# Order of the high and low weight products within a unit, and of the input chunks at the last gate, in a two-block layer on one core

## The chip, the cores and the metric

The kernel runs on one core of one Trainium2 chip. The time is the device time of one execution in microseconds (us), for one launch of the whole program. All times of the trace are counted from the start of the profiled span.

## What is computed

Two transformer blocks follow each other for 256 tokens of width 2048. Nearly all the work is in products of the activations with weights that are read once. What matters for the change, cut from the reference:

```python
# first block
z = h @ w_in                                   # 2048 x 12304
merged = sigmoid(m_a) * (y_a @ w_proj_a) + sigmoid(m_b) * (y_b @ w_proj_b)
y = merged @ w_out
...                                            # cross attention: wq, wk, wv, wo
hid = conv(h @ w_up)                           # 2048 x 11264
y = (gelu(gate) * up) @ w_down                 # 5632 x 2048
# second block
u = h @ w_in_2
q, k, v, z_attn, q_idx, k_idx, w_idx, z_ssd, xbc, dt_raw = split(u)
o_attn = dsa_attention(q, k, v, q_idx, k_idx, w_idx) * silu(z_attn)
o_ssd = ssd_mixer(xbc, z_ssd, dt_raw)          # gated, group-normed
mixed = concatenate([o_attn, o_ssd])           # chunks 0 to 7 and 8 to 15 of 128
out = layer_norm(ALPHA * h + mixed @ w_out_2)
```

## The kernel before, in words

The products keep float32 accuracy from a rounded format: each weight and each activation is held as a high part and a low part. Three products stand for one: high by high, low weight by high activation, high weight by low activation.

**Groups and units.** `groups_of` lists the matrix products as groups of output columns in the order of execution. A group is cut along its input dimension into units of `chunk` times 128 rows (a chunk of the input is 128 rows). A unit is 1 MB of weights in most cases. SyncE loads it into one of three `raw` buffers, ScalarE copies it rounded into `wh` (`split_hi`, semaphore `s_hi`), VectorE subtracts to get `wl` (`split_lo`, semaphore `s_lo`), and TensorE multiplies; at the end of a unit it raises `s_used`, which frees the buffers. ScalarE and VectorE prepare unit n + 2 while TensorE works at n. Units follow the list strictly on every engine.

**Three kinds.** In a "feat" group (256 output columns, units of 8 chunks) the weights are stationary. The activations' high and low halves lie side by side in `xt`, so one product of 512 moving columns does high weight by both parts, and one of 256 columns does low weight by the high part. There are 96 such groups of 16 chunks and 8 of 8 chunks (`pa`), which with two blocks of 128 output columns make 96 x 32 + 8 x 16 = 3200 pairs of one 512-column and one 256-column product. In a "tok" group (512 output columns, units of 4 chunks) the activations are stationary and all three products have 512 moving columns. Of "thin" groups there are two (`glr` and `kiw`), with three products of 256 columns for each chunk.

**The order inside a unit** is written in `block_products` (L940 to L975): for each chunk and block, the high product (or products) and the low product follow each other at once. At a unit's start TensorE waits for `s_lo`, thus for both halves of the weights. In a group's last unit block 0 is finished first, so that its evacuation can begin, and then block 1 (`products`).

**Work beside.** The table `BESIDE` names, for a unit and a slot, what is done between: slot 1 is ahead of unit 1, slot 1.5 is in its middle (on TensorE, ahead of the products of chunk nk // 2). All engines read the same table, so it fixes the order of their queues.

**The end of the second block.** `za0` to `za3` are the four groups of the attention's gate (two units each), `w20` to `w23` the output projection (four units each, input `mix`). The attention part of the mixed input (chunks 0 to 7) comes from `mix_attn`, which multiplies the gate and writes `xth` and `xtl`; it needs the gate's own group finished. The state-space part (chunks 8 to 15) comes from `mix_ssd`: TensorE transposes `xs`, and ScalarE and VectorE copy it scaled into the same `xt`. Both overwrite what `za3` reads, so they wait for `s_used` of `za3`. `ssd_norm` on VectorE finishes `xs` beside `za2`. In the kernel before, `w20` takes its chunks 0 to 15 in order; the two halves of `mix_ssd` stand in the middle of its units 0 and 1.

**Where an input is used first**, `block_products` waits for each chunk by itself (`ready`). Such places that matter here are `xo0` (the output of the cross attention, 4 chunks) and `ug0_0` (the first group of the wide layer; half of its input is transposed at slot 0.5 of its first unit, `h3_b`).

Of the kernel before, what the change touches and what calls it, by code (L numbers as in the profile page):

```python
# [13 lines left out]
KC = D // 128  # L14
# [56 lines left out]
class Group:  # L71


    def __init__(self, name, w, kcs, cols, kind, x, chunk=4, k_off=0, late=0):
        self.name, self.w, self.kcs, self.cols, self.kind, self.x = name, w, kcs, cols, kind, x
        self.chunk, self.k_off, self.late = chunk, k_off, late
        self.width = sum(c for _, c in cols)


class Unit:  # L80


    def __init__(self, n, gi, ui, k, nk, g):
        self.n, self.gi, self.ui, self.k, self.nk, self.g = n, gi, ui, k, nk, g
        self.last = k + nk == g.kcs
        self.m = nk * g.width


# [24 lines left out]
def groups_of(I):  # L113
    w_in, w2, up, down = I["w_in"][0], I["w_in_2"][0], I["ffn_w_up"][0], I["ffn_w_down"][0]
    out = []

    def add(*a, **k):
        out.append(Group(*a, **k))

    for i in range(2):  # L120
        add("vs%d" % i, w_in, KC, [(1024 + 512 * i, 512)], "tok", "h1")
    for i in range(4):
        add("u%d" % i, w_in, KC, [(256 * i, 256)], "feat", "h1", chunk=8)
    for i in range(8):
        add("ma%d" % i, w_in, KC, [(8208 + 256 * i, 256)], "feat", "h1", chunk=8)
    for i in range(8):
        add("pa%d" % i, I["w_proj_a"][0], 8, [(256 * i, 256)], "feat", "ya", chunk=8)
    add("glr", w_in, KC, [(8192, 16)], "thin", "h1", chunk=16)
    for i in range(4):
        add("q%d" % i, w_in, KC, [(2048 + 256 * i, 256)], "feat", "h1", chunk=8)  # L130
    for i in range(4):
        add("k%d" % i, w_in, KC, [(3072 + 256 * i, 256)], "feat", "h1", chunk=8)
    for i in range(4):
        add("v%d" % i, w_in, KC, [(4096 + 512 * i, 512)], "tok", "h1")
    for i in range(4):
        add("og%d" % i, w_in, KC, [(6144 + 512 * i, 512)], "tok", "h1")
    for i in range(8):
        add("mb%d" % i, w_in, KC, [(10256 + 256 * i, 256)], "feat", "h1", chunk=8)
    for i in range(8):
        add("pb%d" % i, I["w_proj_b"][0], KC, [(256 * i, 256)], "feat", "yb", chunk=8)  # L140
    for i in range(4):
        add("wo%d" % i, I["w_out"][0], KC, [(512 * i, 512)], "tok", "mg")
    for i in range(2):
        add("xk%d" % i, I["xa_wk"][0], KC, [(256 * i, 256)], "feat", "mem", chunk=8)
    for i in range(2):
        add("xq%d" % i, I["xa_wq"][0], KC, [(256 * i, 256)], "feat", "h2", chunk=8)
    add("xv", I["xa_wv"][0], KC, [(0, 512)], "tok", "mem")
    for i in range(4):
        add("xo%d" % i, I["xa_wo"][0], 4, [(512 * i, 512)], "tok", "ox", late=3 * (i == 3))
    for half in range(2):  # L150
        for i in range(HF // 2):
            c0 = half * HF * 128 + 256 * i
            add("ug%d_%d" % (half, i), up, KC, [(c0, 256)], "feat", "h3", chunk=8)
            add("uu%d_%d" % (half, i), up, KC, [(FF + c0, 256)], "feat", "h3", chunk=8)
        for i in range(4):
            add("dn%d%d" % (half, i), down, HF, [(512 * i, 512)], "tok", "ac", k_off=half * HF,
                late=2 * (half == 1 and i == 3))
    add("qi0", w2, KC, [(2560, 512)], "tok", "h4")
    add("kiw", w2, KC, [(3584, 80), (6704, 48)], "thin", "h4", chunk=16)
    add("qi1", w2, KC, [(3072, 512)], "tok", "h4")  # L160
    add("kv", w2, KC, [(1024, 512)], "tok", "h4")
    for i in range(8):
        add("xb%d" % i, w2, KC, [(4688 + 256 * i, 256)], "feat", "h4", chunk=8)
    for i in range(2):
        add("q2%d" % i, w2, KC, [(512 * i, 512)], "tok", "h4")
    for i in range(2):
        add("zs%d" % i, w2, KC, [(3664 + 512 * i, 512)], "tok", "h4")
    for i in range(4):
        add("za%d" % i, w2, KC, [(1536 + 256 * i, 256)], "feat", "h4", chunk=8)
    for i in range(4):  # L170
        add("w2%d" % i, I["w_out_2"][0], KC, [(512 * i, 512)], "tok", "mix")
    return out


def units_of(groups):
    units = []
    for gi, g in enumerate(groups):
        for ui, k in enumerate(range(0, g.kcs, g.chunk)):
            units.append(Unit(len(units), gi, ui, k, min(g.chunk, g.kcs - k), g))
    return units  # L180

# [43 lines left out]
}  # L225

# [29 lines left out]
def build(nc, I, cst_d, out_d):  # L256
# [210 lines left out]
    def hi_count(n):  # L467
        return n + 4
# [26 lines left out]
    for stage in plan:  # L495
        for _ in range(BANKS.get(stage, 0) + WARM.get(stage, 0)):
            b = taken % 4
# [55 lines left out]
    def tensor_program(p):  # L553

        def mm(out, l, r, start, stop, share=False):
            return p.matmul(out, l, r, start=start, stop=stop, skip_group_check=share)  # L556
# [383 lines left out]
        def block_products(u, order, begin=True):  # L940

            g, s, nc_ = u.g, u.n % 3, u.g.width
            pset = ps[u.gi % 2]
            xh, xl = operand[g.x]
            h3 = v3(wh[s][:, 0:u.m], nc_)
            l3 = v3(wl[s][:, 0:u.m], nc_)
            if begin and u.n:
                p.wait_ge(s_lo, hi_count(u.n))
            if begin and u.ui == 0 and accfree_base[g.name]:
                p.wait_ge(s_accfree[u.gi % 2], accfree_base[g.name])  # L950
            for b, kk in order:
                if kk == u.nk // 2 and b == 0:
                    run_beside(u, u.ui + 0.5)
                kg = u.k + kk
                if b == 0 and first_use[g.name]:
                    p.wait_ge(*ready(g.x, kg, int(g.k_off > 0)))
                if b == 0 and u.n == 0:
                    p.wait_ge(s_lo, kk + 1)
                first, final = kg == 0, kg == g.kcs - 1
                if g.kind == "tok":  # L960
                    t_ = slice(b * 128, b * 128 + 128)
                    o = pset[b][:, 0:nc_]
                    mm(o, xh[:, kg, t_], h3[:, kk, :], first, False)
                    mm(o, xh[:, kg, t_], l3[:, kk, :], False, False)
                    t = mm(o, xl[:, kg, t_], h3[:, kk, :], False, final)
                elif g.kind == "thin":
                    o = pset[0][0:nc_, 0:256]
                    mm(o, h3[:, kk, :], xh[:, kg, :], first, False)
                    mm(o, h3[:, kk, :], xl[:, kg, :], False, False)
                    t = mm(o, l3[:, kk, :], xh[:, kg, :], False, final)  # L970
                else:
                    c = slice(b * 128, b * 128 + 128)
                    mm(pset[b], h3[:, kk, c], pair(g.x, kg), first, False, share=True)
                    t = mm(pset[b][:, 0:256], l3[:, kk, c], xh[:, kg, :], False, final, share=True)
            return t  # L975

# [32 lines left out]
    def scalar_program(a):  # L1009
# [336 lines left out]
        def mix_attn(tiles):  # L1346
            for i in tiles:
                c = slice(2 * i, 2 * i + 2)
                heard()
                a.wait_ge(s_used, after("za3") - (i < 3))  # L1350
                to_v.add(act(xth[:, c, :], v3(zz[i], 256), ACT.Copy))

        def mix_ssd(k0):
            a.wait_ge(s_used, after("za3"))
            split_turned(use["mix_ssd%d" % k0], lambda k: VT[:, 76 + k:77 + k], k0, xth[:, 8:16, :])

        def evac_w2(i, blocks):
# [120 lines left out]
    def vector_program(v):  # L1478
# [847 lines left out]
        def mix_attn(tiles):  # L2326
            for qb in range(2):
                free(use["at_out%d" % qb][0])
                free(use["at_out%d" % qb][1])
            for i in tiles:  # L2330
                z3 = v3(zz[i], 256)
                c = slice(2 * i, 2 * i + 2)
                heard(last["za%d" % i])
                to_act.add(tt(z3, z3, oaT[:, c, :], ALU.mult))
                heard()
                v.wait_ge(s_used, after("za3") - (i < 3))
                lo_part(xtl[:, c, :], z3, xth[:, c, :]).then_inc(s_mixa, 1)

        def mix_ssd(k0):
            v.wait_ge(s_used, after("za3"))  # L2340
            split_turned(use["mix_ssd%d" % k0], lambda k: VT[:, 76 + k:77 + k], k0, xth[:, 8:16, :], xtl[:, 8:16, :])

        def evac_w2(i, blocks):
# [314 lines left out]
```

## Time and profile before

| | us |
|---|---|
| three runs, median | 2126.94 |
| three runs, lowest and highest | 2124.58, 2134.12 |
| the profiled execution | 2129.74 |
| its span in the trace | 2127.9 |
| mean granted TensorE clock | 0.997 of 2.4 GHz |
| TensorE, products | 2094.1 (98% of the span) |
| TensorE, loading of stationary operands | 1779.3 (84%) |
| VectorE | 1396.8 (66%) |
| ScalarE | 956.1 (45%) |
| DMA queue of the weights | 54.4% of 16 engines |

The profiled execution has 1.84 us outside its span, and is 2.80 us above the median of the three runs. TensorE's busy time is made of modelled ends that overlap (a 512-column product is drawn 0.39 us long and the next one starts after 0.23 us), so the distance from one start to the next is the number that tells what a product costs; it is read from the timeline, or from a window's length over the number of products in it.

### The profile page before, as it was taken

The page shows a single profiled execution, that of the slowest core. Times are in us where ns is not written, and L with a number is a line of the kernel's source. Part 1 is how long each engine was busy: PE and PEld are TensorE (multiplying, and loading weights), DVE is VectorE, ACT ScalarE, POOL GpSimd, SP SyncE. Part 2 cuts the span into 40 slices and gives each one's busy share as a digit, 9 for nine tenths or more (in the row PEclk, how much of TensorE's full clock was granted, in tenths as well). Part 3 has the DMA queues.
Part 4 walks back from the last instruction along what each step waited for, and adds up shares of the span by engine and source line. Part 5 has one row for each costly group of instructions (what it writes and reads, how often), then busy time and mean ns, then how long its engine had stood idle before and what let it go on. Part 6 is the DMA issues. An engine that isn't in the chain of part 4 may idle for free.

```text
span 2127.9 us, 26265 instructions
## 1 busy us (share of the span) xinstructions
PE 2094.1 (98%) x11051; PEld 1779.3 (84%) x11051; DVE 1396.8 (66%) x1566; ACT 956.1 (45%) x927; POOL 26.7 (1%) x42
## 2 busy tenths in 40 slices
PE   8999999999999999999999999999999999999996
PEld 6888888878888888878888888888888888888885
DVE  5665676454556667677777545777754668887765
ACT  5444253234443445464444433444443434445542
POOL 2000000000000000000000000000000000000001
PEclk9999999999999999999999999999999999999998
DMA  8555556445666565445655556556555554554462
GB/s 286 178 183 182 178 159 198 155 162 179 180 190 223 202 234 198 159 133 184 198 179 177 198 189 205 172 185 198 180 203 201 168 178 140 191 165 156 126 238 93
DMA packets 299140, 388.49 MB, mean 183 GB/s; under 512 B 12720, under 2 KB 217860, under 8 KB 297872
## 3 DMA queue, kind: packets, MB, share of 16 engines
q1 hardware_dynamic: 296288, 374.50, 54.4%
q0 software_dynamic: 2560, 12.26, 1.5%
q8 instruction: 87, 1.43, 0.3%
q14 instruction: 29, 0.24, 0.0%
q10 hardware_dynamic: 176, 0.07, 0.0%
HBM read 384.71 MB, written 2.10 MB: 182 GB/s over the span
## 4 chain that ended last, share of the span: by engine, by line
PE 93%; DVE 4%; ACT 1%; issue 1%; DMA 0%; SPq 0%; DVEq 0%; ACTq 0%
PE ps L556 89%; PE pm L556 4%; PE pm L559 1%; DVE wl L1483 1%; ACT wh L1014 1%; DVE y L1483 1%; DMA raw<-in_w_in 0%; DVE xt L1491 0%; DVE vs L1483 0%; ACT xt L1014 0%; DVE yaf L1483 0%; DVE xx L1491 0%; ACT L1014 0%; ACT yaT L1014 0%; DVE uT L1638 0%
## 5 line engine op out<-in xcount | busy, mean ns | idle before, releaser
L1483 DVE TENSOR_TENSOR wl<-raw,wh 128x2048 fp32r<-128x2048 f32 (+1 forms) x361 | 805.0, 2243 | 454.6 <-ACT wh L1014 454.2
L556 PE MATMUL ps<-xt,wh 128*128 128x512 f32 (+2 forms) x2816 | 983.4, 396 | 1.7 <-DVE xt L1491 1.0
L1014 ACT ACTIVATE wh<-raw 128x2048 fp32r<-128x2048 f32 (+1 forms) x361 | 671.2, 1873 | 572.0 <-PE ps L556 567.4
L556 PE MATMUL ps<-xt,wl 128*128 128x256 f32 (+1 forms) x2784 | 779.7, 280 | 0.0
L556 PEld LDWEIGHTS ps<-xt,wh 128*128 128x128 f32 (+1 forms) x2816 | 524.9, 187 | 132.1 <-issue 3.9
L556 PEld LDWEIGHTS ps<-xt,wl 128*128 128x128 f32 (+1 forms) x2784 | 523.8, 188 | 0.5
L556 PE MATMUL ps<-wh,xt 128*128 128x512 f32 x1600 | 504.2, 393 | 1.7 <-DVE xt L1483 1.1
L556 PEld LDWEIGHTS ps<-wh,xt 128*128 128x128 f32 x1600 | 300.5, 188 | 66.5 <-issue 1.8
L556 PE MATMUL ps<-wl,xt 128*128 128x512 f32 x800 | 311.5, 389 | 0.0
L556 PEld LDWEIGHTS ps<-wl,xt 128*128 128x128 f32 x800 | 150.4, 188 | 31.1 <-issue 1.0
L556 PE MATMUL ps<-wh,ach 128*128 128x512 f32 x352 | 137.1, 389 | 0.0
L556 PE MATMUL ps<-wh,acl 128*128 128x512 f32 x352 | 136.9, 389 | 0.0
L556 PE MATMUL ps<-wl,ach 128*128 128x512 f32 x352 | 136.9, 389 | 0.0
L1014 ACT ACTIVATE cv<-up,vt 128x256 f32<-128x256 f32 x88 | 51.3, 602 | 157.4 <-DVE up L1638 157.2
L1491 DVE SCALAR_TENSOR_TENSOR cv<-up,vt,cv 128x255 f32<-128x255 f32 (+1 forms) x176 | 81.2, 482 | 33.0 <-ACT cv L1014 29.8
L556 PE MATMUL ps<-ybT,wh 128*128 128x512 f32 x256 | 88.8, 394 | 0.0
L556 PEld LDWEIGHTS ps<-wh,ach 128*128 128x128 f32 x352 | 66.1, 188 | 13.8
L556 PEld LDWEIGHTS ps<-wh,acl 128*128 128x128 f32 x352 | 66.1, 188 | 13.8
L556 PEld LDWEIGHTS ps<-wl,ach 128*128 128x128 f32 x352 | 66.1, 188 | 13.5
L556 PE MATMUL ps<-ybT,wl 128*128 128x256 f32 x256 | 70.9, 277 | 0.0
L1638 DVE TENSOR_REDUCE up<-ps 128x256 f32<-128x512 f32 x88 | 58.6, 686 | 5.9 <-PE ps L556 5.8
L556 PEld LDWEIGHTS ps<-ybT,wh 128*128 128x128 f32 x256 | 48.0, 188 | 11.1
(323 smaller groups left out, 1366.9 us busy)
## 6 DMA issues: line engine op xcount, KB each, us to landing
raw<-in_w_in SPq DMA_DIRECT2D x147, 1024.0 KB, 5.3
raw<-in_ffn_w_up SPq DMA_DIRECT2D x88, 1024.0 KB, 5.3
raw<-in_ffn_w_down SPq DMA_DIRECT2D x40, 1024.0 KB, 5.1
raw<-in_w_out SPq DMA_DIRECT2D x32, 1024.0 KB, 5.1
raw<-in_w_proj_b SPq DMA_DIRECT2D x16, 1024.0 KB, 5.3
raw<-in_w_proj_a SPq DMA_DIRECT2D x8, 1024.0 KB, 5.3
raw<-in_xa_wk SPq DMA_DIRECT2D x4, 1024.0 KB, 5.1
raw<-in_xa_wq SPq DMA_DIRECT2D x4, 1024.0 KB, 5.2
```

Of the source, the lines that this page charges most:

```text
L556: return p.matmul(out, l, r, start=start, stop=stop, skip_group_check=share)
L559: return p.transpose(out, a, ident)
L1014: return a.activation(out, in_, func, bias=bias, scale=scale)
L1483: return v.tensor_tensor(out, a, b, op)
L1491: return v.scalar_tensor_tensor(out=out, in0=a, scalar=s, in1=b, op0=op0, op1=op1)
L1638: v.tensor_reduce(out, halves, AX.X, ALU.add).then_inc(s_accfree[set_of[name]], 1)
```

## The change

Inside a unit, all products with the high weights come first, for all chunks and blocks of the call, and then all products with the low weights. TensorE waits for `s_hi` at the unit's start and for `s_lo` between the two halves. In "tok" groups the high half thus has two products for each chunk and block, the low half one. The number of products, loads and columns is the same. A group's first product is now told by the unit and not by the chunk number, so that chunks can be taken in another order.

`za3` and `w20` take the input chunks 8 to 15 first. `mix_ssd` moves from the middle of units 0 and 1 of `w20` to the start and the middle of `za3`'s second unit, and waits for one unit less of `za3`; `mix_attn0` moves to `w20`'s unit 0 and `mix_attn3` to its unit 1.

```diff
@@ class Unit
-        self.last = k + nk == g.kcs
+        self.last = (ui + 1) * g.chunk >= g.kcs
@@ groups_of
-        add("za%d" % i, w2, KC, [(1536 + 256 * i, 256)], "feat", "h4", chunk=8)
+        add("za%d" % i, w2, KC, [(1536 + 256 * i, 256)], "feat", "h4", chunk=8, k_first=8 * (i == 3))
...
-        add("w2%d" % i, I["w_out_2"][0], KC, [(512 * i, 512)], "tok", "mix")
+        add("w2%d" % i, I["w_out_2"][0], KC, [(512 * i, 512)], "tok", "mix", k_first=8 * (i == 0))
@@ units_of
-        for ui, k in enumerate(range(0, g.kcs, g.chunk)):
+        for ui, k in enumerate(list(range(g.k_first, g.kcs, g.chunk)) + list(range(0, g.k_first, g.chunk))):
@@ BESIDE
-    ("za3", 1): ["mix_attn0"], ("w20", 0): ["mix_attn3"], ("w20", 0.5): ["mix_ssd0"], ("w20", 1.5): ["mix_ssd4"],
+    ("za3", 1): ["mix_ssd0"], ("za3", 1.5): ["mix_ssd4"], ("w20", 0): ["mix_attn0"], ("w20", 1): ["mix_attn3"],
@@ tensor_program, block_products
             if begin and u.n:
-                p.wait_ge(s_lo, hi_count(u.n))
+                p.wait_ge(s_hi, hi_count(u.n))
...
                 if b == 0 and u.n == 0:
+                    p.wait_ge(s_hi, kk + 1)
+                first = u.ui == 0 and kk == 0
+                t_, c = slice(b * 128, b * 128 + 128), slice(b * 128, b * 128 + 128)
+                if g.kind == "tok":
+                    mm(pset[b], xh[:, kg, t_], h3[:, kk, :], first, False)
+                    mm(pset[b], xl[:, kg, t_], h3[:, kk, :], False, False)
+                elif g.kind == "thin":
+                    mm(pset[0][0:nc_, 0:256], h3[:, kk, :], xh[:, kg, :], first, False)
+                    mm(pset[0][0:nc_, 0:256], h3[:, kk, :], xl[:, kg, :], False, False)
+                else:
+                    mm(pset[b], h3[:, kk, c], pair(g.x, kg), first, False, share=True)
+            if begin and u.n:
+                p.wait_ge(s_lo, hi_count(u.n))
+            for b, kk in order:
+                kg = u.k + kk
+                if b == 0 and u.n == 0:
                     p.wait_ge(s_lo, kk + 1)
-                first, final = kg == 0, kg == g.kcs - 1
+                final = u.last and kk == u.nk - 1
+                t_, c = slice(b * 128, b * 128 + 128), slice(b * 128, b * 128 + 128)
                 if g.kind == "tok":
...
-                    mm(o, xh[:, kg, t_], h3[:, kk, :], first, False)
-                    mm(o, xh[:, kg, t_], l3[:, kk, :], False, False)
-                    t = mm(o, xl[:, kg, t_], h3[:, kk, :], False, final)
+                    t = mm(pset[b], xh[:, kg, t_], l3[:, kk, :], False, final)
...
                 else:
...
-                    mm(pset[b], h3[:, kk, c], pair(g.x, kg), first, False, share=True)
                     t = mm(pset[b][:, 0:256], l3[:, kk, c], xh[:, kg, :], False, final, share=True)
@@ scalar_program and vector_program, mix_attn (a. and v.)
-                a.wait_ge(s_used, after("za3") - (i < 3))
+                a.wait_ge(s_used, after("za3"))
@@ scalar_program and vector_program, mix_ssd (a. and v.)
-            a.wait_ge(s_used, after("za3"))
+            a.wait_ge(s_used, after("za3") - 1)
```

## Rows read from the trace of the kernel before

**Rows 1.** The page, busy time, share of the span, instructions.

```profile
PE 2094.1 (98%) x11051; PEld 1779.3 (84%) x11051; DVE 1396.8 (66%) x1566; ACT 956.1 (45%) x927; POOL 26.7 (1%) x42
```

**Rows 2.** The page, chain that ended last, shares by engine.

```profile
PE 93%; DVE 4%; ACT 1%; issue 1%; DMA 0%; SPq 0%; DVEq 0%; ACTq 0%
```

**Rows 3.** The chain in order of time, wide layer: start, us, what.

```profile
937.47 728.64 PE ps L556 x3832
```

**Rows 4.** Windows: stretch, length, then busy (x count) by engine, PEclk, DMA.

```profile
280.00:340.00 60.00, 60.00 (x342) 51.99 (x341) 46.49 (x40) 29.91 (x16) 0.00 (x0) 1.00 0.58 177
...
600.00:720.00 120.00, 120.00 (x694) 104.93 (x693) 78.17 (x64) 45.48 (x31) 1.09 (x2) 1.00 0.65 209
950.00:1170.00 220.00, 220.00 (x1247) 190.80 (x1246) 160.66 (x174) 106.35 (x97) 0.00 (x0) 1.00 0.57 183
1200.00:1290.00 90.00, 90.00 (x398) 74.51 (x397) 41.38 (x24) 32.18 (x19) 0.00 (x0) 1.00 0.58 194
1310.00:1540.00 230.00, 230.00 (x1305) 199.40 (x1304) 167.68 (x181) 109.04 (x101) 0.00 (x0) 1.00 0.56 183
```

**Rows 5.** Timeline, TensorE, the thin group kiw: start, us, what.

```profile
1703.62 0.28 PE L556 MATMUL ps<-xt,wl 128*128 128x256 f32 x1
1703.74 0.40 PE L556 MATMUL ps<-xt,wh 128*128 128x256 f32 x2
...
1709.03 0.28 PE L556 MATMUL ps<-xt,wl 128*128 128x256 f32 x1
```

**Rows 6.** Timeline, TensorE, the thin group glr.

```profile
250.35 0.40 PE L556 MATMUL ps<-xt,wh 128*16 128x256 f32 x2
...
251.06 0.40 PE L556 MATMUL ps<-xt,wh 128*16 128x256 f32 x2
```

**Rows 7.** Timeline, TensorE, unit starts between 92 and 138 us.

```profile
92.81 0.28 PE L556 MATMUL ps<-xt,wl 128*128 128x256 f32 x1
93.47 0.51 PE L556 MATMUL ps<-xt,wh 128*128 128x512 f32 x1 [0.38 <-DVE wl L1483]
93.81 0.28 PE L556 MATMUL ps<-xt,wl 128*128 128x256 f32 x1
...
99.11 0.28 PE L556 MATMUL ps<-xt,wl 128*128 128x256 f32 x1
99.46 0.50 PE L556 MATMUL ps<-xt,wh 128*128 128x512 f32 x1
...
136.72 0.28 PE L556 MATMUL ps<-xt,wl 128*128 128x256 f32 x1
137.19 0.50 PE L556 MATMUL ps<-xt,wh 128*128 128x512 f32 x1 [0.18 <-DVE wl L1483]
```

**Rows 8.** Timeline, VectorE and TensorE, from the last gate into the output projection.

```profile
2008.41 2.36 DVE L1483 TENSOR_TENSOR xs<-xs,st 128x1024 f32<-128x1024 f32 x2
...
2018.89 0.68 DVE L1483 TENSOR_TENSOR zk<-zk,oaT 128x512 f32<-128x512 f32 x1
...
2020.88 0.69 DVE L1483 TENSOR_TENSOR zk<-zk,oaT 128x512 f32<-128x512 f32 x1
...
2021.12 0.47 PE L556 MATMUL ps<-wh,xt 128*128 128x512 f32 x1
...
2030.74 0.60 PE L559 MATMUL pm<-cst,xs 128*128 128x128 f32 x4
...
2032.13 0.50 PE L556 MATMUL ps<-wh,xt 128*128 128x512 f32 x1 [0.79 <-DVE xt L1483]
```

**Rows 9.** Timeline, TensorE, first units of ug0_0 and of xo0.

```profile
934.38 0.28 PE L556 MATMUL ps<-xt,wl 128*128 128x256 f32 x1
935.04 0.30 PE L559 MATMUL pm<-cst,yA 128*128 128x128 f32 x1 [0.39 <-DVE yA L1487]
...
900.58 0.40 PE L556 MATMUL ps<-wh,oxl 128*128 128x512 f32 x1
900.99 0.51 PE L556 MATMUL ps<-wh,oxh 128*128 128x512 f32 x1
```

More of the change, by code:

```diff
@@ L71, with __init__ @@
 class Group:
-    def __init__(self, name, w, kcs, cols, kind, x, chunk=4, k_off=0, late=0):
+    def __init__(self, name, w, kcs, cols, kind, x, chunk=4, k_off=0, late=0, k_first=0):
         self.name, self.w, self.kcs, self.cols, self.kind, self.x = name, w, kcs, cols, kind, x
-        self.chunk, self.k_off, self.late = chunk, k_off, late
+        self.chunk, self.k_off, self.late, self.k_first = chunk, k_off, late, k_first
         self.width = sum(c for _, c in cols)
@@ L957, in block_products @@
                 if b == 0 and u.n == 0:
+                    p.wait_ge(s_hi, kk + 1)
[14 more added lines that the diff above has]
+                if b == 0 and u.n == 0:
                     p.wait_ge(s_lo, kk + 1)
-                first, final = kg == 0, kg == g.kcs - 1
+                final = u.last and kk == u.nk - 1
+                t_, c = slice(b * 128, b * 128 + 128), slice(b * 128, b * 128 + 128)
                 if g.kind == "tok":
-                    t_ = slice(b * 128, b * 128 + 128)
-                    o = pset[b][:, 0:nc_]
-                    mm(o, xh[:, kg, t_], h3[:, kk, :], first, False)
-                    mm(o, xh[:, kg, t_], l3[:, kk, :], False, False)
-                    t = mm(o, xl[:, kg, t_], h3[:, kk, :], False, final)
+                    t = mm(pset[b], xh[:, kg, t_], l3[:, kk, :], False, final)
                 elif g.kind == "thin":
[L967 to L970, printed above, removed]
-                else:
-                    c = slice(b * 128, b * 128 + 128)
-                    mm(pset[b], h3[:, kk, c], pair(g.x, kg), first, False, share=True)
+                    t = mm(pset[0][0:nc_, 0:256], l3[:, kk, :], xh[:, kg, :], False, final)
+                else:
                     t = mm(pset[b][:, 0:256], l3[:, kk, c], xh[:, kg, :], False, final, share=True)
@@ L2335, in mix_attn @@
                 heard()
-                v.wait_ge(s_used, after("za3") - (i < 3))
+                v.wait_ge(s_used, after("za3"))
                 lo_part(xtl[:, c, :], z3, xth[:, c, :]).then_inc(s_mixa, 1)
         def mix_ssd(k0):
-            v.wait_ge(s_used, after("za3"))
+            v.wait_ge(s_used, after("za3") - 1)
             split_turned(use["mix_ssd%d" % k0], lambda k: VT[:, 76 + k:77 + k], k0, xth[:, 8:16, :], xtl[:, 8:16, :])
```

## The prediction

> **What bounds the kernel now.** I read the page first. TensorE is busy for 98% of the span, VectorE for 66% [rows 1], and the chain that ended last lies on TensorE for 93% [rows 2]. So a change can gain in two ways: the few waits of TensorE go, or a product costs less. A product's cost is not its drawn length. It is the distance between starts, and a window over a stretch of products alone gives it: length over count, less the two or so that lap over the edges.
>
> A stretch of 512-column products gives 90.00 / 396.5 = 0.227 us each. For the pairs of the feat groups (one of 512 and one of 256 columns) four windows give 60 / 340 = 0.1765, 220 / 1245 = 0.1767 and 230 / 1303 = 0.1765 us a product, thus 0.353 a pair, but 120 / 692 = 0.1734, or 0.3467 a pair, between 600 and 720 us; the granted clock is 1.00 in all [rows 4]. The same pair has two prices. What would the two cost apart? The only 256-column products in a row with a 128-column load ahead of each are those of kiw: from 1703.62 to 1709.03 there are 15 triples, 5.41 / 45 = 0.1202 us each [rows 5]. And 0.2267 + 0.1202 = 0.3469: the cheaper price is the sum of the parts, and the dearer one has 0.0066 us on top, which comes with the alternation, since neither the runs of 512 columns nor those of 256 show it.
>
> **The change part by part.**
>
> *Grouping by length (feat).* It neither adds nor removes a product or a load: 3200 pairs, in half-units of up to 16 equal products. Price after: 0.2267 for a high product. In the trace such runs have activations stationary and weights moving, here it is the other way round; I take the same price, because the pair's own sum fits. For a low product, bounds: kiw's 0.1202, and below it glr's 0.1183 (from 250.35 to 251.06, six products [rows 6]), which has 16 stationary columns and is thus less like. The other end is no gain, the pair at 0.353. I take kiw's, since shape and load are the same. Gain: I let the window at 280 us stand for u, ma, pa, q and k (20 groups of 32 pairs and 8 of 16: 768) and those at 950 and 1310 us for ug and uu (44 groups: 1408), in all 2176 x 0.0066 = 14.4 us. The other 1024 pairs are at the cheap price where the window at 600 us looks, and the dear price must end somewhere ahead of it; I add a guess of 0.9. So **15.3 us**, ends 0 and, with glr's price, 15.3 + 3200 x 0.0019 = 21.4.
>
> By the Trainium skill, "TensorE: Matmul & The Clock Gate", section "Back-to-back issue gap", a product costs its columns over 2.4 GHz and 2.5 ns. An estimate from that page is 0.216 + 0.109 = 0.325 us a pair in any order, so that grouping gives nothing; the trace disagrees with both numbers, since it has 0.347 and 0.353.
>
> *Grouping in tok.* All three products have 512 columns before and after, 0.227 each. Nothing; the end on either side is a hundredth of a microsecond a unit, 3 us at most, since in the long stretches all neighbours of such a product have its length already.
>
> *The second wait in each unit.* 361 units now have one more wait. What is queued behind it is only TensorE's own low half. A wait that is already fulfilled costs nothing where rows show it: the 3832 products from 937.47 to 1666.11 contain 135 unit starts, each with its wait, and at 0.353 a pair and 0.227 a product the stretch is filled to about 0.1 us [rows 3, 4]. Behind a wait that does hold, the next product starts about 0.11 us late as well (93.47 to 93.81 is 0.34 in place of 0.23 [rows 7]). I take 0; ends 0 and 361 x 0.11 = 40 us.
>
> *Waiting for the high weights only.* Three unit starts are late because of `wl`: 93.47, 99.46 and 137.19 [rows 7]. Against the 0.12 of the low product before them they lose 0.54, 0.23 and 0.35, and 0.11 each behind. After the change `wl` is wanted 16 x 0.227 = 3.6 us later, so these **1.4 us** go. VectorE stays as loaded as it was, so what is late next there is its evacuations, and they have nobody waiting within that half unit.
>
> *The last gate and w20.* TensorE stands from about 2031.2 (four transposes from 2030.74 on, 0.11 each) to 2032.13, and loses 0.11 behind it: it wants chunks 6 and 7 of the mixed input, which VectorE writes last [rows 8]. After, w20 begins with chunks 8 to 15. Moved: two times 8 transposes on TensorE, 8 copies each on ScalarE and VectorE, no DMA; `xs` is ready at 2008.41 + 2.36 = 2010.8, and za3's second unit starts at 2021.12 - 5.55 = 2015.6, so the transposes don't wait. The copies are queued on VectorE ahead of `wl` for w20's unit 1, which is wanted some 9 us after w20's start. mix_attn then has the two units 0 and 1, 24 x 0.227 = 5.4 us each, for four tiles whose products on VectorE follow each other by 2.0 us (2018.89 to 2020.88 [rows 8]) and two splits between. Gain **1.0 us**. The loads of the last norm's vectors on POOL's queue wait for mix_ssd4 and start earlier, which nobody needs. If VectorE were later than that, unit 2 of w20 would wait in the place of unit 1.
>
> *What is lost.* A half-unit of high products runs through the chunks faster than before, so an input that is late is met sooner, and the low products that used to fill the time come after it. At ug0_0 the transposes of slot 0.5 wait for `yA` until 935.04 [rows 9]; four chunks' low products, 8 x 0.12 = 1.0 us, no longer lie ahead of them. At xo0 two low products of 0.23 move behind the wait that ends at 900.99 [rows 9]: 0.4 us. Together **1.4 us lost**.
>
> Sum: 15.3 + 1.4 + 1.0 - 1.4 = **16.3 us**. The profiled execution of 2129.74 (span 2127.9 and 1.84 around it) would come to 2113.4. It lies 2.80 above the median of the runs, and against that the forecast is 2126.94 - 16.3 = **2110.6**.
>
> **The rivals.**
>
> *A: the pair keeps its price.* The 0.0066 us might not come from alternation but from something else of these stretches, and go with high runs just the same. For it: the same alternation is cheap at 600 us [rows 4], so alternation alone does not make it, and the page's order-free rule would also give no gain. Against it: tok runs at 1200 us, between two dear stretches, are at 0.227 [rows 4]. Then only the waits and the losses are left, 1.4 + 1.0 - 1.4 = 1.0, and the time is 2125.9.
>
> *B: the second wait costs.* The middle wait parts the loading ahead of the low products from the high ones in front. If each costs the 0.11 us of a fill, it is 40 us, and the time 2126.94 - 16.3 + 40 = 2151. The side flips to slower by over 0.5% (10.6 us) from (16.3 + 10.6) / 361 = 0.075 us a wait. Against it stands the stretch of 135 waits at no cost [rows 3].
>
> *C: the low half is bound by its loads.* Each low product needs a fresh load, drawn 1779.3 / 11051 = 0.161 us long on average [rows 1]; in a run there is no 512-column product to hide it. If a low product took 0.161, it would be 3200 x 0.041 = 131 us more, and 2242. kiw's 0.120 speaks plainly against it [rows 5]. By the Trainium skill, same page, section "LDWEIGHTS (loading the stationary operand)", a load of 128 columns takes an estimated 107 ns; kiw's step is above that and cannot part the load from the product.
>
> **How the numbers follow.** The forecast has 0.74, with an own range from 2106 to 2116 (glr's price on one side, a third of the gain missing on the other). A has 0.15, B 0.08, C 0.02, and 0.01 is left for the order at the end turning into a longer wait. A measurement of this kernel can tell about 0.5%, 10.6 us. Faster by more than that takes the forecast to hold for at least two thirds, 0.75; the same 0.15 (A), slower 0.10 (B and C). The forecast's own range holds about 0.7, so to hold 8 in 10 the range has to reach to A: 2105 to 2126.5.
>
> **What would show it.** In the changed profile a window within 950 to 1160 should have 0.1734 us a product, and the timeline low products in runs of 0.120 and high ones in runs of 0.227. The first low product behind the last high one should start 0.227 after it; 0.34 there means B. The wait at 2032 should be gone, those on `wl` before 140 us too, and the one on `yA` near 935 about 1 us longer. A pair still at 0.353 means A. The forecast is wrong if the chain shows TensorE in one piece through the wide layer and the piece is not about 9 us shorter than 728.6.

## The result and the profile after

The change made the kernel faster, by a little less than half of what was forecast (7.6 us between the medians, 16.3 forecast): the median of 11 runs is 2122.14 us (2119.56 to 2122.74), that of the kernel before in 11 runs 2129.78 (2123.17 to 2134.12). The ratio is 0.9963, with a 95% interval of 0.9952 to 0.9974, thus 0.26% to 0.48% faster, where the forecast was 2110.6 us or 0.8%. The profiled execution took 2122.14 us, its span is 2120.4. Two things strike at once. The gain is within the 0.5% that the forecast called "the same", and the runs of the kernel before are spread over 11 us, those of the changed one within 3.2. The size of the gain depends on these runs: the kernel before was run again beside the experiments, 25, 17 and 11 times, with medians of 2127.29, 2127.91 and 2129.38 us, and the changed kernel's median lies 5.2 to 7.2 us below those.

The page of the changed kernel, busy times and the chain's shares [rows 1, 2]:

```profile
PE 2086.7 (98%) x11051; PEld 1788.6 (84%) x11051; DVE 1395.0 (66%) x1566; ACT 953.8 (45%) x927; POOL 26.5 (1%) x42
...
PE 97%; DVE 2%; DMA 0%; ACT 0%; issue 0%; SPq 0%; DVEq 0%; ACTq 0%
```

TensorE has 97% of the chain instead of 93%. That is not a measure of time saved: the waits found gone below come to some 2.4 us, a tenth of a per cent of the span, so most of the four points are a chain that takes another way through the same work. What the kernel's time hangs on is TensorE's own pace.

The windows of the changed kernel, with the columns of [rows 4]:

```profile
280.00:340.00 60.00, 60.00 (x344) 52.80 (x343) 47.08 (x41) 30.24 (x17) 0.00 (x0) 1.00 0.60 182
600.00:720.00 120.00, 120.00 (x686) 105.64 (x686) 76.78 (x64) 46.12 (x33) 1.09 (x2) 1.00 0.65 210
950.00:1160.00 210.00, 210.00 (x1207) 185.22 (x1206) 154.62 (x168) 101.12 (x94) 0.00 (x0) 1.00 0.58 186
```

And the wide layer in its chain in order of time [rows 3]:

```profile
936.48 722.88 PE ps L556 x3840
```

210 / 1205 = 0.1743 us a product is 0.3485 a pair. The forecast's test was 0.1734, or 0.3467. The piece of the chain is 5.8 us shorter than the 728.64 of before, where the forecast's sign was about 9. The counts at 280 and 600 us give 0.3509, which is too dear: such a window begins and ends inside runs, and the one at 600 us holds 348 long products but 337 short ones. A group's start and the next one's are surer, here two pb groups in TensorE's timeline of the changed kernel:

```profile
649.33 3.82 PE L556 MATMUL ps<-ybT,wh 128*128 128x512 f32 x16
...
660.48 0.86 PE L556 MATMUL ps<-ybT,wh 128*128 128x512 f32 x3
```

11.15 us for 32 pairs is 0.3485 there too, **dearer** than the 0.3467 of before. So the grouped order has one price in all these stretches, between the two that the kernel before had.

Where the missing 0.0018 a pair sits shows the timeline of the changed kernel, TensorE, from one unit of the wide layer into the next. Each row is a run of equal products; its cost is the distance to the next start, not the drawn length:

```profile
1001.42 3.82 PE L556 MATMUL ps<-xt,wh 128*128 128x512 f32 x16
1005.08 2.08 PE L556 MATMUL ps<-xt,wl 128*128 128x256 f32 x16
1006.99 2.00 PE L556 MATMUL ps<-xt,wh 128*128 128x512 f32 x8
1008.83 1.11 PE L556 MATMUL ps<-xt,wl 128*128 128x256 f32 x8
```

The 16 high products take 3.66 us and not 3.627 (16 x 0.2267), the 8 take 1.84 and not 1.813: both 0.03 too long, whatever the run's length. The low runs take 1.91 and 0.95, a hundredth less than 16 and 8 times 0.120. In the single starts of the trace, read to the nanosecond, the first five high products behind a low run of 8 or 16 are 0.234, 0.236, 0.228, 0.232 and 0.231 apart, and from the sixth on 0.227; the first low product follows after 0.227 and is itself 0.007 short. So a **passage** from low products to high ones costs 0.028 - 0.007 = 0.021 us net. A group of two units has three, 0.06 us: 32 x 0.3467 + 0.06 = 11.153 us, which is what every full feat group of the changed kernel takes that follows another one and has no wait or other work in it.

The waits. At 93 and at 99 us the high products now follow at once, [rows 7] had 0.54 and 0.23 us there:

```profile
92.77 1.36 PE L556 MATMUL ps<-xt,wl 128*128 128x256 f32 x10
93.97 2.00 PE L556 MATMUL ps<-xt,wh 128*128 128x512 f32 x8
...
98.60 1.11 PE L556 MATMUL ps<-xt,wl 128*128 128x256 f32 x8
99.55 0.63 PE L556 MATMUL ps<-xt,wh 128*128 128x512 f32 x2
```

The step from 92.77 to 93.97 is ten low products at 0.120. The last gate passes into w20 without a break (TensorE's timeline; [rows 8] had the transposes at 2030.74 and the wait up to 2032.13):

```profile
2009.18 1.03 PE L559 MATMUL pm<-cst,xs 128*128 128x128 f32 x8
2009.97 1.17 PE L556 MATMUL ps<-xt,wh 128*128 128x512 f32 x4
2010.98 1.04 PE L559 MATMUL pm<-cst,xs 128*128 128x128 f32 x8
...
2015.57 1.11 PE L556 MATMUL ps<-xt,wl 128*128 128x256 f32 x8
2016.52 3.82 PE L556 MATMUL ps<-wh,xt 128*128 128x512 f32 x16
```

The two losses came as worked out: at ug0_0 and at xo0 TensorE now waits where low products had lain [rows 9]:

```profile
899.53 0.49 PE L556 MATMUL ps<-wh,oxh 128*128 128x512 f32 x1 [0.47 <-DVE oxl L1491]
...
934.05 0.30 PE L559 MATMUL pm<-cst,yA 128*128 128x128 f32 x1 [1.33 <-DVE yA L1495]
```

And one thing that was not in the forecast: in the window from 262 us the granted clock is 0.72 on average.

```profile
262.00:268.00 6.00, 6.00 (x23) 4.73 (x22) 4.12 (x6) 0.69 (x1) 0.00 (x0) 0.72 0.44 125
```

From 264.0 to 267.4 it was at its lower level (1.2 GHz), and products of 512 columns were 0.427 apart. Ahead of it TensorE had run two lots of four small products (gate2_2 and gate2_3, 256 columns each) with only four high products between. Five other profiled executions have the same order there (e2, e4, e5, e6, e8 below) and did not fall there. The same steps of 0.427 stand at the very start, from 17.2 to 21.7, where the kernel before was at 0.227 from 17.6 on.

**The account between the two profiled executions**, by group starts: up to 66 us 1.45 lost (the slow start); 66 to 248 us 3.6 gained (pairs from 0.353 to 0.3485, and the three waits); to 270 us 1.3 lost (the clock); to 580 us 1.4 gained; 580 to 728 us 0.8 **lost** (0.3467 to 0.3485); xo0 and ug0_0 0.5 and 0.9 lost; the wide layer's rest 3.2 and 3.4 gained; xb 0.4 lost; the end 1.2 gained. Together 7.5, the difference of the spans.

### The profile page after: what moved, and what is told of

Read it like the earlier page. It is cut to its first block, busy times and chain, and to the rows that moved or that the text cites. A ratio compares the mean times of both kernels' runs of the same rounds, so it can differ in the third digit from the quotient of the medians.

```text
span 2120.4 us, 26265 instructions
## 1 busy us (share of the span) xinstructions
PE 2086.7 (98%) x11051; PEld 1788.6 (84%) x11051; DVE 1395.0 (66%) x1566; ACT 953.8 (45%) x927; POOL 26.5 (1%) x42
## 4 chain that ended last, share of the span: by engine, by line
PE 97%; DVE 2%; DMA 0%; ACT 0%; issue 0%; SPq 0%; DVEq 0%; ACTq 0%
PE ps L556 92%; PE pm L556 4%; PE pm L559 1%; DVE y L1491 1%; DMA raw<-in_w_in 0%; DVE xx L1499 0%; DVE xt L1499 0%; ACT junkB L1042 0%; ACT xt L1022 0%; DVE wl L1491 0%; DVE yA L1495 0%; SPq L2532 0%; ACT y L1022 0%; DVE xt L1491 0%; DVE bst L2361 0%
## 5 line engine op out<-in xcount | busy, mean ns | idle before, releaser
L556 PE MATMUL ps<-xt,wh 128*128 128x512 f32 (+2 forms) x2816 | 684.7, 390 | 1.0 <-DVE xt L1499 1.0
L556 PEld LDWEIGHTS ps<-xt,wh 128*128 128x128 f32 (+1 forms) x2816 | 507.5, 188 | 98.1 <-issue 3.9
L556 PE MATMUL ps<-wh,xt 128*128 128x512 f32 x1600 | 390.6, 394 | 0.9 <-DVE xt L1499 0.5
L556 PEld LDWEIGHTS ps<-xt,wl 128*128 128x128 f32 (+1 forms) x2784 | 368.4, 191 | 20.6
L556 PE MATMUL ps<-xt,wl 128*128 128x256 f32 (+1 forms) x2784 | 375.1, 283 | 0.0
L556 PE MATMUL ps<-wl,xt 128*128 128x512 f32 x800 | 201.9, 389 | 0.0
L556 PE MATMUL ps<-wl,ach 128*128 128x512 f32 x352 | 89.0, 389 | 0.0
L556 PE MATMUL ps<-ybT,wh 128*128 128x512 f32 x256 | 62.6, 391 | 0.0
L1022 ACT ACTIVATE ach<-cv 128x512 fp32r<-128x512 f32 x22 | 13.9, 632 | 59.7 <-DVE cv L1491 59.7
```

The costliest lines, as they stand in the source:

```text
L1022: return a.activation(out, in_, func, bias=bias, scale=scale)
```

## The experiments

Two theories for the pair were put on record. S: the price sits at the passages from low products to high ones. P: every low product is dearer than taken. When the first runs were in, a second question took over, why the old order has two prices. M: it is set by how TensorE enters a stretch and then kept. N: chance or DMA traffic. In the code cuts a run length of 0 means all high products and then all low ones, 1 one by one as before, and -1 the low ones first. e4, e5, e7 and e9 were executed once each, so they are read by their traces and not by their times.

**e1_end_order.** The kernel before with only the end of the change.

All units are in the old order; of the change it has `k_first` for `za3` and `w20` and the new places in `BESIDE`, with their waits.

> Old order of the products in every unit; only the order of the chunks in za3 and w20 and the places of mix_ssd and mix_attn are the change's. Theory S (what is left of the expected gain was lost where a run of 256-column products is followed by 512-column ones, and at the clock in two places) and theory P (every low product of a grouped unit is dearer than taken) both expect 1.0 us less than before and no wait at the start of w20's unit for the mixed input; everything up to za3 is as before.

Measured: median 2128.56 us in 10 runs, ratio 1.0000 (0.9986 to 1.0013). One microsecond can't be seen against runs that lie from 2123.6 to 2133.8, but the trace settles this part, and against the expectation. From za3's first product to w21's it takes 36.90 us, 1.0 **more** than the 35.88 of before, where the change has 34.69. The wait at w20's start is gone, but unit 2 of w20 now waits for its low weights, which VectorE writes behind the tiles of `mix_attn`. The end of its chain in order of time, and the same product in TensorE's timeline:

```profile
2026.41 2.29 DVE wl L1483
2028.75 71.03 PE ps L556 x312
...
2028.75 0.50 PE L556 MATMUL ps<-wh,xt 128*128 128x512 f32 x1 [1.91 <-DVE wl L1483]
```

The new order of the chunks alone thus loses 1.0 us here; it gains only together with the grouped tok order, which wants the low weights of a unit 3.6 us later.

The expectation "as before up to za3" failed too: the profiled execution took 2123.62 us, and its wide layer was 4.6 us shorter than before with the same instructions. Its chain in order of time:

```profile
934.99 724.04 PE ps L556 x3832
```

Its windows:

```profile
140.00:200.00 60.00, 60.00 (x348) 52.44 (x347) 31.77 (x22) 25.99 (x18) 0.51 (x1) 1.00 0.67 205
950.00:1160.00 210.00, 210.00 (x1213) 185.19 (x1212) 155.62 (x171) 99.20 (x95) 0.00 (x0) 1.00 0.59 191
```

210 / 1211 is 0.1734, the cheap price, in the stretch that was dear in the profile of before. The old order's price differs between executions.

**e2_feat_grouped.** The change, with tok and thin groups in the old order.

```diff
+        def run_length(u, second):
+            return 0 if u.g.kind == "feat" else "old"
```

> The change with tok and thin groups in the old order (high, low, high with one wait for the low weights at the start). If unit 0's slow clock in the changed kernel (steps of 0.427 us up to 21.8) comes from its new order, this one has steps of 0.227 from about 17.6 on and h1_c's transposes start near 22.5 instead of 24.7: about 2 us faster than the change, span near 2118. If the late clock there is chance, it is within 0.7 us of the change. The feat windows show 0.349 a pair as in the change under both theories.

Measured: 2122.46 us, ratio 0.9983 (0.9973 to 0.9992), within 0.4 us of the change's median. The slow clock at the start is there as well, up to 20.5, though unit 0 has the old order; so it is not made by the order of unit 0, and the 2 us expected from that did not come. In its profile the clock fell at other places, at 928.5 and 2027.6. Feat groups without other work are at 0.3485 a pair. Its w20 has the wait of e1: 1.87 us for the low weights of unit 2.

**e3_tok_grouped.** The reverse: feat old, tok and thin grouped.

```diff
+        def run_length(u, second):
+            return "old" if u.g.kind == "feat" else 0
```

> The change with feat groups in the old order, tok and thin grouped. Both theories: feat pairs at 0.347 or 0.353 as before, tok products at 0.227, so no gain from the grouping; with the end's 1.0 us, and if the slow start is made by the new order of unit 0, 2 us lost: a span of 2127 to 2129. If grouping of tok had brought a part of the gain, the span would be below 2125.

Measured: 2126.51 us, ratio 0.9998 (0.9986 to 1.0009). The span of the profiled execution is 2124.7, below the 2125 that was to show a gain from grouping tok, but it can't be read so: its wide layer is at the cheap price, worth 4.6 us against before. By the starts a tok product costs 0.227 as before (29.92 us for a group of `dn` in both), so the price has no part in it. Yet the grouping does bring something in one place: w20 takes 21.77 us, where e1 has 23.97 with its wait. That is 2.2 us, for the 0.5 that it loses at xo0. The profile is dear between 140 and 200, where e1 was cheap, and cheap from 950 as e1 was. The chain in order of time:

```profile
938.47 724.03 PE ps L556 x3832
```

Its windows:

```profile
140.00:200.00 60.00, 60.00 (x342) 52.00 (x341) 32.60 (x23) 24.21 (x17) 0.51 (x1) 1.00 0.66 208
950.00:1160.00 210.00, 210.00 (x1213) 183.68 (x1212) 154.05 (x167) 101.76 (x95) 0.00 (x0) 1.00 0.58 187
```

**e7_before_again.** The kernel before, not changed at all.

> The kernel before, unchanged, to see its pair price in another execution. Theory M: 0.3533 between 1310 and 1540 and 0.3467 between 600 and 720 as in all profiles so far, since the way into these stretches has no wait on another engine; between 950 and 1170 and between 60 and 340, which are entered after such waits, either price, and the execution's time follows: 2129 to 2131 with both dear, 2122 to 2125 with the one at 950 cheap. Rival: the same prices as in the first profile of this kernel everywhere.

Its one execution took 2128.6 us. Its chain in order of time:

```profile
936.40 728.64 PE ps L556 x3832
```

Its windows:

```profile
140.00:200.00 60.00, 60.00 (x348) 52.49 (x347) 32.64 (x23) 25.12 (x18) 0.51 (x1) 1.00 0.67 208
600.00:720.00 120.00, 120.00 (x694) 104.94 (x693) 77.40 (x65) 46.73 (x33) 1.09 (x2) 1.00 0.65 210
```

With this the four combinations are together, each in one profiled execution with the old order in all feat groups:

| kernel | 110 to 250 us | 945 to 1180 us | execution, us |
|---|---|---|---|
| e1 | cheap | cheap | 2123.62 |
| e3 | dear | cheap | 2126.49 |
| e7 | cheap | dear | 2128.6 |
| before | dear | dear | 2129.74 |

A dear group takes 11.31 us where a cheap one takes 11.093. Over the first stretch that makes 2.5 us (from u3's start at 99.5 to glr's start 150.9 us in the kernel before and 148.4 in e1), over the second 4.6, 7.1 together. That is most of the 11 us over which the runs of the kernel before lie; that the other executions, of which no trace was kept, differ in the same way is argued and not shown, and the clock has a part as well. Both stretches begin behind a wait on VectorE (at 99, and at 935). The stretches behind none, 280 to 350, 600 to 728 and 1302 to 1551, have the same price in all four: dear, cheap, dear.

The single starts tell the two prices apart. In mb5 of the kernel before (cheap) the long products are 0.230 to 0.233 and the short ones 0.112 to 0.118 apart, and a pair of 0.343 follows one of 0.350. In ug0_5 (dear) the pairs come in threes, 0.350, 0.350 and 0.360. So in alternation neither product has the price that it has in a run.

**e4_runs.** Other run lengths in the wide layer.

```diff
+RUNS = {"0_1": 1, "0_2": 1, "0_3": 2, "0_4": 2, "0_5": 4, "0_6": 4, "0_7": 8, "0_8": 8, "0_9": -1, "0_10": -1, ...}
```

> The change with other run lengths in the feat groups of the wide layer: ug/uu 0_1, 0_2, 1_0, 1_1, 1_4, 1_5 alternate one by one, 0_3, 0_4, 1_8, 1_9 two by two, 0_5, 0_6, 1_2, 1_3 four by four, 0_7, 0_8 eight by eight, and 0_9, 0_10, 1_6, 1_7 take the low half first in block 0 of the second unit, which leaves out one of three passages from low to high. Theory S: the price sits at the passage and is about 0.021 net after a run of eight or more; eight by eight 0.3493 a pair, four by four between 0.349 and 0.352, two by two up to 0.357, one by one 0.347 or 0.353, and low first the passages' 0.021 less per group. Theory P: 0.349 a pair for all runs of two and more, and low first gains nothing.

Its one execution took 2120.83 us. The starts of the first ug group of each kind in the first half, four groups (ug and uu) to each row of TensorE's timeline:

```profile
953.19 0.40 PE L556 MATMUL ps<-xt,wh 128*128 128x512 f32 x1
998.43 0.62 PE L556 MATMUL ps<-xt,wh 128*128 128x512 f32 x2
1043.01 0.63 PE L556 MATMUL ps<-xt,wh 128*128 128x512 f32 x2
1087.90 0.63 PE L556 MATMUL ps<-xt,wh 128*128 128x512 f32 x2
1132.60 0.63 PE L556 MATMUL ps<-xt,wh 128*128 128x512 f32 x2
1177.13 0.40 PE L556 MATMUL ps<-wh,ach 128*128 128x512 f32 x1
```

Over four: 11.310 us one by one, 11.145 by twos, 11.223 by fours, 11.175 by eights, 11.133 low first. The floor is 32 x 0.3467 = 11.093. The second half gives the same for ones, twos, fours and low first. Per passage from low to high that is 0.007, 0.003, 0.016, 0.020 and 0.020. S holds and P falls: by P twos, fours and eights would cost the same, and low first would gain nothing. But S too was wrong at the short end, where twos are cheaper than fours: a passage costs 0.016 us in runs of four, and 0.02 only from runs of eight on.

**e5_entry.** The ug groups of the wide layer in different runs, with a group of the change's order (first half) or of twos (second half) between.

```diff
+PROBE = [1, (2, 1), (2, 2, 1), (3, 1), (1, 2, 1), (4, 1), 3, 2, "lag", (6, 2), 5]
```

> The change, with the ug groups of the wide layer (but the first) in other run lengths and a group of the change's order (half 0) or of runs of two (half 1) between. ug_0: one by one; ug_1, 2, 3, 4, 5: a first run of 2, of 2 and 2, of 3, of 1 and 2, of 4, and then one by one to the group's end; ug_6: threes; ug_7: twos; ug_8: the low product one place late (H H L H L ...); ug_9: 6 and then twos; ug_10: fives. Theory M (the price of one-by-one order is set by how the run of it is entered, and then kept): some entries give groups of 11.09 us (0.3467 a pair), others 11.31 (0.3533), the same entry the same in both halves where what stands ahead is the same. Theory N (chance, or something outside TensorE such as the DMA traffic): the price changes within groups or does not follow the entry. Twos 11.15 as in the run before; threes between 11.15 and 11.23.

Its one execution took 2121.62 us. Its starts of groups in TensorE's timeline, first half (ug0_1, uu0_1, ug0_2, uu0_2), then second half (ug1_0, uu1_0, ug1_1, uu1_1):

```profile
953.93 0.63 PE L556 MATMUL ps<-xt,wh 128*128 128x512 f32 x2
965.03 0.62 PE L556 MATMUL ps<-xt,wh 128*128 128x512 f32 x2
976.17 0.63 PE L556 MATMUL ps<-xt,wh 128*128 128x512 f32 x2
987.45 0.64 PE L556 MATMUL ps<-xt,wh 128*128 128x512 f32 x2
...
1296.86 0.39 PE L556 MATMUL ps<-xt,wh 128*128 128x512 f32 x1
1308.14 0.64 PE L556 MATMUL ps<-xt,wh 128*128 128x512 f32 x2
1319.31 0.63 PE L556 MATMUL ps<-xt,wh 128*128 128x512 f32 x2
1330.40 0.62 PE L556 MATMUL ps<-xt,wh 128*128 128x512 f32 x2
```

ug0_1, a run of two and then one by one: 11.10 us. ug0_2, two runs of two and then one by one: 11.28. ug1_0, one by one from its first product: 11.29. ug1_1, a run of two first: 11.10. So the same 28 or 30 alternating pairs have either price by what stands ahead of them, and keep it to the group's end. Of the other beginnings (3, 1 and 2, 4) each was near 11.11 in the first half and near 11.29 in the second, where twos and not the change's order stood ahead. Late low products (ug_8) took 11.246 and 11.288, twos and "6 and then twos" 11.127 to 11.147, as expected of twos. Threes took 11.204 in both halves, fives 11.225 and 11.207, all dearer than the change's 11.153. And what stands ahead matters, not the beginning alone: two runs of two gave 11.28 in the first half and 11.10 in the second. M holds, but without the rule that would tell the price in advance.

**e9_two_first.** Every feat group begins with a run of two and goes on one by one.

```diff
+            if u.g.kind != "feat":
+                return 0
+            return (2, 1) if u.ui == 0 and not second else 1
```

> The change with every feat group one by one but for a run of two at its start. Theory M: each group enters anew from the state in which the one ahead left it, so that a stretch falls into a regular pattern of prices between 11.09 and 11.31 us a group, the same in the stretch from 1300 on as in the one from 945 on, or each constant. Theory N: an irregular pattern.

Four starts of groups in TensorE's timeline:

```profile
955.97 0.62 PE L556 MATMUL ps<-xt,wh 128*128 128x512 f32 x2
967.27 0.63 PE L556 MATMUL ps<-xt,wh 128*128 128x512 f32 x2
978.37 0.62 PE L556 MATMUL ps<-xt,wh 128*128 128x512 f32 x2
989.66 0.63 PE L556 MATMUL ps<-xt,wh 128*128 128x512 f32 x2
```

11.30, 11.10, 11.29, and so on without an exception from 945 to 1180 and again from 1311 to 1546: a run of two in the middle of alternating pairs turns the dear price into the cheap one and the cheap one into the dear. M, in its regular form. One place does not follow: the half-size groups pa1 to pa7 begin with a run of two as well and are all dear (5.647 us, cheap is 5.547), so the switch is no rule for every group. The execution took 2125.12 us.

**e6_low_first.** The change, with block 0 of each second unit taking its low products first.

```diff
+return -1 if u.g.kind == "feat" and u.ui == 1 and not second and not first_use[u.g.name] else 0
```

> The change, with block 0 of the second unit of each feat group (but those where an input is used first) taking its low products first, so that low follows low and one of three passages from low to high goes. From the run with other run lengths: 11.133 in place of 11.153 us a group, thus some 90 x 0.02 = 1.8 us less than the change: median near 2120.3, ratio to the kernel before near 0.9965. If the passages are not what is left, it is 2122 as the change.

Measured: 2119.46 us in 12 runs (2117.53 to 2123.17), ratio 0.9965 (0.9954 to 0.9977). The median is where it was expected, but the ratio is that of the change (0.9963), so the times tell nothing, and the place is in part luck: at 92.6 TensorE now waits for low weights that it wants at the start of u2's second unit, 1.0 us that was not expected. The chain shows the passages: the wide layer is 0.86 us shorter than the change's 722.88, for 43 groups 0.020 each.

```profile
932.99 722.02 PE ps L556 x3840
```

**e8_keep_cheap.** One by one, entered on purpose: the change's order behind each wait and tok group, a run of two, and then alternating pairs to the end of the stretch.

```diff
+place = {"ma": i - 4, "pa": 1 + i, "mb": i - 1, "pb": 1 + i, "q": i - 2, "k": 1 + i}.get(name[:-1], -1)
+if name[:2] in ("ug", "uu"): place = 2 * i + (name[1] == "u") - 1 - (name[2] == "0")
+if u.g.kind != "feat" or place < 0: return 0
+return (2, 1) if place == 0 and u.ui == 0 and not second else 1
```

> One by one again in most feat groups, but entered on purpose: the change's order in each group that follows a wait or a tok group, then one group that begins with a run of two, and one by one from there to the end of the stretch (ma4 to pa7, q2 to k3, mb1 to pb7, ug0_1 to uu0_10, uu1_0 to uu1_10). Theory M: 0.3467 a pair in all of these in every execution, 11.093 us a group in place of the change's 11.153, so 67 groups x 0.06 = 4 us less than the change: median near 2118, and a narrow spread like the change's. Theory N: some of these stretches at 0.3533, and a spread of 8 us or more over the executions as in the kernel before.

Measured: 2114.18 us in 6 runs (2114.01 to 2119.57), ratio 0.9940 (0.9926 to 0.9954), thus 0.6% faster than the kernel before. The changed kernel was not run beside it; its ratio was 0.9963 (0.9952 to 0.9974), and the two intervals just touch. Its chain in order of time:

```profile
931.00 720.38 PE ps L556 x3840
```

Its windows:

```profile
950.00:1160.00 210.00, 210.00 (x1215) 183.73 (x1214) 154.36 (x172) 101.21 (x95) 0.00 (x0) 1.00 0.59 190
1310.00:1530.00 220.00, 220.00 (x1271) 192.38 (x1270) 164.00 (x179) 104.80 (x98) 0.00 (x0) 1.00 0.58 188
```

220 / 1269 = 0.1734 where the kernel before had 0.1765 in both its profiles. The groups meant are at 11.093 to 11.098 us and the halves at 5.547; only mb1 to mb3, which have other work in them, take longer. Against the change that is 66 groups of 0.06 and 8 halves of 0.04, 4.3 us, in the one execution that was profiled. The median came out 4 us below what was expected: in the profile the clock was at the higher level from 16.3 us, 5.4 earlier than in the change's, and did not fall again before the end, which is worth about 3.7 us and is not the edit's doing as far as these runs show. The spread is not the narrow one that was expected: four runs lie within 0.2 us, the other two are 3.6 and 5.4 us longer, at a mean clock of 0.994 in place of 0.996 or 0.997. A share of 0.002 of 2114 us is some 4 us, so the lower clock accounts for most of that; no trace of these two was kept.

## Why the prediction was wrong

**The step that failed is the price after in "Grouping by length"**: 15.3 us forecast for the term, and by the group starts 9.4 between the two profiled executions, 10.2 gained in u, ma, pa, q, k, ug and uu and 0.8 lost in the other feat groups, most of which were cheap. Two things in the step were wrong, and only the first makes this shortfall.

*The price after.* It was taken as the sum 0.2267 + 0.1202, each product's price in a run of its own kind, and the passages between the runs were put at nothing. That sum holds inside runs, but three passages a group (two in a half) cost 0.02 each: 304 passages, 6.1 us, which is all of the difference between 15.3 and 9.4. The evidence was taken from one side only: kiw shows short products alone, and no row showed long products behind short ones in a run. That the sum came out at the cheap price of the pair is luck: in alternation both products cost something else (e7 above), and only the mean is the same.

*The price before.* "It comes with the alternation" was wrong, and rival A had named the reason, that the same alternation is cheap at 600 us. The dear price comes with the entry and stays; in two stretches it differs between executions, and the one execution profiled had both dear. For that execution 15.3 us was right (9.4 and 6.1 are 15.5); for one with both cheap it would be 7.1 less. e1, which has both cheap, took 2123.62 us, 1.5 more than the changed kernel's 2122.14, although e1 lost 1.0 at the end and the changed one 3.0 to the clock.

*The whole.* The profiled execution was to come to 2113.4 and took 2122.14. Of these 8.7 us the passages are 5.9 and the clock 3.0, and the other terms are right to 0.2 us each. The median lies outside the forecast's own range of 2106 to 2116, and inside the wide one only because that was drawn out to rival A. A's 2125.9 is nearer (3.8 us off, the forecast 11.5), but its mechanism did not come true: the price of the pair did change in every feat group.

*The second wait*: taken at 0, and 0 it is. The first low product behind the last high one follows after 0.227 us throughout; rival B has no trace. (The kernel has 358 units, not 361, which changes nothing.) *Rival C*: low products are 0.120 apart in runs of 16, so loads don't bind them.

*The waits for the low weights* are gone: 1.4 forecast, 1.2 found. So is the one at w20: 1.0 forecast, 1.2 found at the end. The worry put beside that term, that unit 2 of w20 would wait instead, is what e1 and e2 show; the grouped tok order covers it. *The losses* were 0.5 at xo0 and 0.9 at ug0_0, forecast 1.4 together. *Tok*: the price is unchanged as forecast, and the term missed the 2.2 us at w20 that the end's gain rests on.

*The clock* had no place in the sum. In the change's profile it took back about 3 us, at the start and at 264. e2 has the slow start with unit 0 in the old order, e7, the unchanged kernel, fell to the lower level at 930, and e8 has neither. e3, e4, e5, e6, e8 and e9 have the new order of unit 0 and are at the higher level from 16 to 19 us on. So it varies by execution; the fall at 264 was seen in one of six profiled executions with that order there, too few to say whether the change makes it likelier.

The formula cited from the Trainium skill, "TensorE: Matmul & The Clock Gate", section "Back-to-back issue gap", is given there for a product by itself, and the section says that in a stream of loads and products the distance is another; it has no term for order, and "order-free" was the prediction's own reading of it. The estimate of 0.325 us a pair in any order does not fit these runs: the same 64 products of a group took 11.093 to 11.311 us by order and by entry, at the full clock.

## What to carry to other kernels

Before a term is built on a price per instruction, see whether the same instructions have that price in a second profiled execution; a kernel whose runs are spread over 11 us and whose trace shows two prices for one pattern is telling that they don't. When products of unlike length are regrouped, count the passages and not only the products, and measure one. An order whose price does not depend on the entry is worth something by itself, and an order that depends on it can be entered on purpose. And when two parts of a change are tried apart, read the stretch in the trace: here the new end without the grouped order was a loss, which ten runs could not show.

## What the runs showed of the hardware

Behind eight or sixteen products of 256 moving columns, the first five of 512 columns start 0.007, 0.009, 0.002, 0.005 and 0.004 us late (0.227 is the step in a run), 0.028 in all, of which 0.007 comes back at the passage to short ones. It is the same for tok products behind a feat group (2016.52 in the changed kernel). Strict alternation has two steady states, 0.3467 and 0.3533 us a pair, each held for over 200 us. The cheap one repeats every two pairs, the dear one every three. In the full-size groups of e9 a single run of two in its midst switches from one to the other; in the half-size groups pa1 to pa7 it does not. What in TensorE or in its loads keeps the state is open.
